# Two of 32 expert weight loads split into nine partition-strided DMAs

## The chip, the core and the metric

The kernel runs on one core of one Trainium2 chip. The metric is the device time of one execution in microseconds; a comparison takes medians of several runs. The core has a matrix engine (TensorE, PE in the profile), a vector engine (DVE), a scalar engine (ACT), GpSimd (POOL), a sync engine (SP) that here only issues loads, and 16 DMA engines that move data between HBM and the on-chip memory SBUF, which has 128 partitions.

## The reference, cut to what matters

One block of a transformer on 256 tokens of width 1024, all in float32: a mixer (two attentions, gates, an output projection, about the first fifth of the time) and then a mixture of 32 experts, of which each token takes 4. The kernel computes the experts one after the other, each on up to 64 gathered tokens, so it reads all weights of all experts once:

```python
def expert_block(args):
    xb, e = args
    hgu = xb @ w_gu[e] + b_gu[e]                     # w_gu[e]: 1024 x 2048 float32, 8 MB
    gate = jnp.minimum(hgu[:, :D_EXPERT], SWIGLU_LIMIT)
    up = jnp.clip(hgu[:, D_EXPERT:], -SWIGLU_LIMIT, SWIGLU_LIMIT)
    act = (up + 1.0) * gate * jax.nn.sigmoid(SWIGLU_ALPHA * gate)
    return act @ w_down[e] + b_down[e]               # w_down[e]: 1024 x 1024 float32, 4 MB
```

Here 1 MB is 2^20 bytes. 32 experts times 12 MB are 384 MB of the 436.72 MB (of 10^6 bytes) that the page counts, 402.7 of them in its unit.

## The kernel before

Program order is written out by hand for each engine. For expert `e` PE multiplies the gathered tokens with `w_gate_up` (line 1019, 64 matmuls), then with `w_down` (line 1033, 32 matmuls). Each of the two weights has two places in SBUF, one for even and one for odd experts: `gate_up_room`, and `even_down` / `odd_down`. A place is 128 partitions wide; for experts 6 to 27 partition `p` of a `w_down` place holds rows 8p to 8p+7 of the matrix, 32 KB that also lie in one piece in HBM (`dn_rows`).

SP issues all weight loads in one order: gate_up of expert e, then down of expert e, then e+1, and so on (`load_gate_up`, `load_down`). Before each it waits until PE has finished with expert e-2, which used the same place (`released`: semaphore `m_gu` for gate_up, `m_y` for down). Once a load has been issued it stands in the queue of the 16 DMA engines; SP goes on without waiting for its end.

A load says that it is done through a semaphore of its place (`full`), which rises by 16 per transfer. PE waits in `piece` until that semaphore has the sum of all transfers up to this expert; `full_count` computes the sum from `signals(e, i)`, the number of transfers for piece `i` of expert `e`. For `w_down` of experts 6 to 27 that number was 1 for the first half (`i == GU`) and 0 for the second, as one transfer brings both.

The middle of the program has a break before expert 16, where SP, DVE and ACT look at the largest token count of an expert, and where the biases of all experts are added. The last two experts' `w_down` come in halves and quarters, so that PE can begin before all has landed.

Of the kernel before, what the change touches and what calls it, by code (L numbers as in the profile page):

```python
# [25 lines left out]
P = 128  # L26
# [15 lines left out]
GU, DN = 4, 2  # L42
# [3 lines left out]
EIGHT = range(6, 28)  # L46
JOINED = tuple(e for e in range(6, 26) if e not in (15, 18))
BREAK = 16
OB = SEQ // SLOTS - 1
FF = 1024  # L50
EPS = 1e-6
# [86 lines left out]
def hybrid_block(nc, x, xt, w_in, gain_rows, head_rows, w_proj_a, w_proj_b, w_out,  # L138
                 w_router, w_gate_up, b_gate_up, w_down, b_down, consts, out):
    with ExitStack() as ctx:  # L140
# [208 lines left out]
        def whole_rows(e):  # L349

            return w_gate_up[0, e].rearrange("(p h) n -> p (h n)", h=KC)
# [12 lines left out]
        def dn_rows(e):  # L364

            return w_down[0, e].rearrange("(p h) n -> p (h n)", h=8)
# [9 lines left out]
        downs = [even_down[:, 0:8192], odd_down[:, 2048:10240]]  # L376

        def place(e, i):

            if i >= GU:  # L380
                return downs[e % 2][:, (i - GU) * 4096:(i - GU + 1) * 4096]
            return quads[e % 2 * 2 + i // 2][:, (i % 2) * 4096:(i % 2 + 1) * 4096]

        def full(e, i):
            return place_full[e % 2 * TURNS + i]

        def signals(e, i):

            if i < GU and e in JOINED:
                return 1 if i == 0 else 0  # L390
            if e in (WHOLE if i < GU else EIGHT):
                return 1 - i % 2
            return 2 if (e, i) in ((0, 5), (1, 4), (1, 5), (2, 0)) else 1

        def full_count(e, i):

            return 16 * sum(signals(n, i) for n in range(e % 2, e + 1, 2))

        def by_rows(e):

            return e != 0 and e != BREAK

# [24 lines left out]
        def _(sp):  # L427
# [33 lines left out]
            def load(e, i, done=None):  # L461
                sp.dma_start(place(e, i), source(e, i)).then_inc(done or full(e, i), 16)
# [28 lines left out]
            def released(e, i):  # L491

                if i < GU - 1:
                    sp.wait_ge(gu_used, (e - 2) * (GU - 1) + i + 1)
                elif i == GU - 1:
                    sp.wait_ge(m_gu, e - 1)
                elif i < TURNS - 1:
                    sp.wait_ge(dn_used, (e - 2) * (DN - 1) + i - GU + 1)
                else:
                    sp.wait_ge(m_y, e - 1)  # L500

            def load_gate_up(e):

                if e in JOINED:
                    released(e, GU - 1)
                    sp.dma_start(wholes[e % 2], whole_rows(e)).then_inc(full(e, 0), 16)
                    return
                for d in range(2):
                    if e in WHOLE:
                        released(e, 2 * d + 1)  # L510
                        load_quad(e, d)
                        continue
                    for i in (2 * d, 2 * d + 1):
                        if (e, i) == (2, 0):
                            sp.wait_ge(gu_first, 1)
                            load_half(e, i, 0)
                            released(e, i)
                            load_half(e, i, 1)
                        else:
                            released(e, i)  # L520
                            load(e, i)

            def load_down(e):

                if e in EIGHT:
                    released(e, TURNS - 1)
                    sp.dma_start(downs[e % 2], dn_rows(e)).then_inc(full(e, GU), 16)
                    return
                for i in range(GU, TURNS):
                    released(e, i)  # L530
                    load(e, i)
# [24 lines left out]

            for e in range(2, BREAK + 2):
                load_gate_up(e)
                load_down(e)
# [3 lines left out]
            with sp.If(most > SLOTS):  # L563
                for i in range(TURNS):
                    sp.wait_ge(full(BREAK, i), full_count(BREAK, i))
                with sp.Fori(0, NE) as e:
                    sp.wait_ge(o_pe, e * (6 * OB) + 1)
                    for i in range(GU):
                        sp.dma_start(place(BREAK, i), whole_rows(e)[:, i * 4096:(i + 1) * 4096]).then_inc(o_full, 16)
                    for s in range(DN):  # L570
                        sp.dma_start(place(BREAK, GU + s), dn_rows(e)[:, s * 4096:(s + 1) * 4096]).then_inc(o_full, 16)
                sp.wait_ge(o_pe, NE * 6 * OB + 1)
                for i in range(TURNS):
                    load(BREAK, i, o_full)

            for e in range(BREAK + 2, NE - 2):
                load_gate_up(e)
                load_down(e)
# [50 lines left out]
        def _(pe):  # L629
# [421 lines left out]
            def piece(e, i):  # L1051

                if signals(e, i):
                    pe.wait_ge(full(e, i), full_count(e, i))
                return place(e, i)
# [23 lines left out]
            def overflow():  # L1079

                with pe.Fori(0, NE) as e:
                    with pe.Fori(0, OB) as j:
                        n = e * OB + j
                        pe.wait_ge(o_dve, n * 5 + 1)
# [121 lines left out]
        def _(dve):  # L1206
# [425 lines left out]
            def overflow():  # L1632

                dve.wait_ge(m_gt, BREAK)
                with dve.Fori(0, NE) as e:
                    with dve.Fori(0, OB) as j:
                        n = e * OB + j
                        dve.wait_ge(o_pe, n * 6 + 1)
# [256 lines left out]
```

## Time and profile before

| | us |
|---|---|
| median of 3 runs (1127.17 to 1127.55) | 1127.24 |
| the profiled execution | 1131.17 |
| its span, first to last instruction | 1129.4 |
| PE busy | 1089.1 |
| DVE busy | 293.7 |
| ACT busy | 136.3 |

The profiled execution is 3.93 us longer than the median, and 1.8 us longer than its own span. The page cuts the span in 40 slices of 28.2 us; "DMA" is the mean busy share of the 16 DMA engines in tenths, "GB/s" what they moved, "PEclk" the granted TensorE clock. A PE that waits inside a stream of pipelined matmuls can still look busy, so a 9 in its line does not say that it sets the pace. "Landing" is the time from the issue of a transfer on SP to the last of its data.

### The profile page before, as it was taken

How to read it: one execution, taken by the hardware profiler on the slowest of the kernel's cores; microseconds unless marked ns; L12 is line 12 of the kernel's file. 1: busy time of each engine (PE TensorE's matmuls, PEld its weight loads, DVE VectorE, ACT ScalarE, POOL GpSimd, SP SyncE). 2: the span in 40 equal slices, each digit the busy share in tenths (PEclk: the TensorE clock that was granted, in tenths of full speed). 3: DMA queues.
4: the chain of work that ended last, by engine and by line, in shares of the span. 5: the costliest groups of instructions: out<-in, count | busy, mean ns of one | idle time of the engine just before them, and what ended most of it. 6: DMA issues, size and time to landing. Idle time of an engine off the chain costs nothing.

```text
span 1129.4 us, 11872 instructions
## 1 busy us (share of the span) xinstructions
PE 1089.1 (96%) x5275; PEld 481.4 (43%) x5275; DVE 293.7 (26%) x677; ACT 136.3 (12%) x232; POOL 8.3 (1%) x16
## 2 busy tenths in 40 slices
PE   9999999999999999999999968999999999999997
PEld 5678897533333333333333324333333333333332
DVE  2788742331111111121111110212111111111111
ACT  1425340110000000000000000100000000000001
POOL 0100000000000000000000000000000000000000
PEclk9999999999999999999999987999999999999999
DMA  8533488699999999999999999999999999999996
GB/s 313 231 150 138 161 319 357 263 400 402 430 428 438 439 430 425 435 435 428 435 430 424 436 420 426 430 429 436 427 433 430 433 432 430 431 424 428 427 424 261
DMA packets 21652, 436.72 MB, mean 387 GB/s; under 512 B 2496, under 2 KB 2880, under 8 KB 6272
## 3 DMA queue, kind: packets, MB, share of 16 engines
q1 hardware_dynamic: 21072, 435.27, 91.1%
q8 instruction: 43, 0.70, 0.3%
q10 hardware_dynamic: 528, 0.68, 0.2%
q14 instruction: 9, 0.07, 0.0%
HBM read 434.89 MB, written 1.05 MB: 386 GB/s over the span
## 4 chain that ended last, share of the span: by engine, by line
PE 79%; DMA 17%; DVE 3%; issue 1%; SPq 1%; ACT 0%; ACTq 0%; DVEq 0%
PE Pp L1019 33%; PE Bp L1033 14%; DMA gate_up_room<-in_w_gate_up 12%; PE Pp L701 4%; PE Ap L1047 4%; DMA odd_down<-in_w_down 3%; PE Bp L1005 3%; PE Pp L650 3%; PE Pp L666 2%; PE Pp L901 2%; PE Ap L912 2%; PE Bp L1026 1%; PE Pp L690 1%; DVE odd_down L1630 1%; DMA odd_down<-in_b_down 1%; PE Pp L961 1%
## 5 line engine op out<-in xcount | busy, mean ns | idle before, releaser
L1019 PE MATMUL Pp<-gate_up_room,OBT 128*64 128x512 f32 x2048 | 453.4, 601 | 13.8 <-DMA gate_up_room<-in_w_gate_up 13.8
L1019 PEld LDWEIGHTS Pp<-gate_up_room,OBT 128*64 128x64 f32 x2048 | 147.0, 139 | 303.7 <-issue 279.9
L1619 DVE TENSOR_SCALAR odd_down<-Pp 128x512 f32<-128x512 f32 x31 | 21.4, 692 | 618.2 <-PE Pp L1019 618.2
L1033 PE MATMUL Bp<-even_down,odd_down 128*64 128x512 f32 x512 | 113.7, 595 | 1.2
L1033 PE MATMUL Bp<-odd_down 128*64 128x512 f32 x480 | 106.3, 595 | 1.8 <-DVE odd_down L1630 0.6
L1820 ACT ACTIVATE odd_down<-odd_down 128x512 f32<-128x512 f32 x30 | 18.9, 630 | 476.0 <-DVE odd_down L1619 476.0
L1047 PE MATMUL Ap<-odd_down,cst 64*128 64x512 f32 x256 | 65.4, 630 | 5.2 <-DMA odd_down<-in_b_down 4.5
L1033 PEld LDWEIGHTS Bp<-even_down,odd_down 128*64 128x64 f32 x512 | 35.2, 137 | 69.1 <-issue 63.3
L1033 PEld LDWEIGHTS Bp<-odd_down 128*64 128x64 f32 x480 | 33.1, 137 | 65.3 <-issue 59.9
L1005 PE MATMUL Bp<-X,cst 128*64 128x512 f32 x240 | 56.6, 592 | 0.0
L701 PE MATMUL Pp<-odd_down,gate_up_room 128*128 128x128 f32 x448 | 53.2, 277 | 0.5 <-DVE odd_down L1370 0.5
L701 PEld LDWEIGHTS Pp<-odd_down,gate_up_room 128*128 128x128 f32 x448 | 51.1, 192 | 2.5 <-issue 1.3
L1832 ACT ACTIVATE odd_down<-Bp 128x512 f32<-128x512 f32 x30 | 17.9, 597 | 204.3 <-PE Bp L1033 204.3
L1047 PEld LDWEIGHTS Ap<-odd_down,cst 64*128 64x128 f32 x256 | 22.6, 190 | 46.2 <-issue 44.6
L650 PE MATMUL Pp<-gate_up_room,odd_down 128*128 128x512 f32 (+1 forms) x96 | 33.5, 507 | 0.0
L1630 DVE COPY odd_down<-Bp 128x512 f32<-128x512 f32 x31 | 21.4, 691 | 44.6 <-PE Bp L1026 44.6
L1005 PEld LDWEIGHTS Bp<-X,cst 128*64 128x64 f32 x240 | 17.1, 137 | 34.4 <-issue 34.4
L1026 PEld LDWEIGHTS Bp<-cst,odd_down 128*128 128x128 f32 x128 | 17.8, 208 | 26.3 <-DVE odd_down L1626 26.3
L666 PE MATMUL Pp<-odd_down,gate_up_room 128*128 128x256 f32 x128 | 28.2, 380 | 0.0
L912 PE MATMUL Ap<-gate_up_room,odd_down 128*128 128x512 f32 x64 | 28.1, 592 | 0.0
L1026 PE MATMUL Bp<-cst,odd_down 128*128 128x128 f32 x128 | 23.7, 307 | 3.2 <-DVE odd_down L1626 3.2
L666 PEld LDWEIGHTS Pp<-odd_down,gate_up_room 128*128 128x128 f32 x128 | 24.1, 190 | 3.5 <-issue 0.3
(227 smaller groups left out, 698.3 us busy)
## 6 DMA issues: line engine op xcount, KB each, us to landing
gate_up_room<-in_w_gate_up SPq DMA_DIRECT2D x14, 4096.0 KB, 23.6
gate_up_room<-in_w_gate_up SPq DMA_DIRECT2D x27, 2048.0 KB, 42.7
even_down<-in_w_down SPq DMA_DIRECT2D x11, 4096.0 KB, 36.0
odd_down<-in_w_down SPq DMA_DIRECT2D x11, 4096.0 KB, 39.6
gate_up_room<-in_w_in SPq DMA_DIRECT2D x8, 2048.0 KB, 7.4
even_down<-in_w_down SPq DMA_DIRECT2D x7, 2048.0 KB, 17.5
odd_down<-in_w_down SPq DMA_DIRECT2D x6, 2048.0 KB, 21.1
odd_down<-in_w_down SPq DMA_DIRECT2D x7, 1024.0 KB, 21.6
```

The lines of the kernel that those rows point to most:

```text
L650: last = mm(bank[:, 0:n], XT[:, k, b * P:(b + 1) * P], uview(u, n)[:, k, :], start=k == 0, stop=k == KC - 1)
L666: last = mm(bank[:, t * SEQ:(t + 1) * SEQ], uview(u)[:, k, c:c + P], XT[:, k, :], start=k == 0, stop=k == KC - 1)
L701: last = mm(Pp[:, t % 2, part * P:(part + 1) * P], w[:, k, f], x[:, k, :], start=start and k == 0, stop=stop and k == 3, skip_group_check= ...
L901: last = mm(Pp[:, c % 2, ab * SEQ:(ab + 1) * SEQ], urows(u)[:, j, c * P:(c + 1) * P], o[:, j, :], start=j == 0, stop=j == NP2 - 1)
L912: last = mm(Ap[:, 2 * b + hf, :], XT[:, c, b * P:(b + 1) * P], out_cols(hf)[:, c, :], start=c == 0, stop=c == KC - 1)
L1005: last = mm(out_bank[64 * r:64 * r + 64, :], OH[:, b, :], part, start=b == 0, stop=b == 1, skip_group_check=True)
L1019: last = mm((Gps, Ups)[q // 2][64 * (q % 2):64 * (q % 2) + 64, :], xT[:, k % 4, k // 4, :], quarter(e, w, q), start=False, stop=k == KC - ...
L1026: last = tr(bank[:, c * P:(c + 1) * P], act_fours[:, c, :], ident)
L1033: last = mm(bank[64 * hf:64 * hf + 64, :], turned[:, c, s, :], w[:, c * 1024 + hf * 512:][:, 0:512], start=s == 0 and c == 0, stop=s == DN ...
L1047: last = mm(Ap[:, 2 * b + hf, :], gates[h, b * P:(b + 1) * P], results[h, :], start=start, stop=stop, skip_group_check=True)
L1619: V.tensor_scalar(gm, Gps, LIMIT, None, ALU.min).then_inc(d_gm, 1)
L1630: V.tensor_copy(hTf, Yps).then_inc(d_ht, 1)
```

## The change

`w_down` of experts 12 and 22, both in `even_down`, no longer comes as one transfer of 128 rows (partitions) of 32 KB. It comes as nine: seven of 16 rows each, which take partitions r, r+8, r+16, ... for r from 0 to 6, and two of eight rows each, which take partitions 7, 23, 39, ... and 15, 31, 47, .... Together they write the same bytes to the same places. `signals` says 9 for these two, so PE waits for all nine. Everything else stands as it was; four lines go into `load_down`, and lines behind them move by 3 to 8.

```diff
--- before.py
+++ after.py
@@ -46,6 +46,7 @@
 EIGHT = range(6, 28)
 JOINED = tuple(e for e in range(6, 26) if e not in (15, 18))
 BREAK = 16
+UNEVEN = (12, 22)
 OB = SEQ // SLOTS - 1
 FF = 1024
 EPS = 1e-6
@@ -388,6 +389,8 @@
 
             if i < GU and e in JOINED:
                 return 1 if i == 0 else 0
+            if i == GU and e in UNEVEN:
+                return 9
             if e in (WHOLE if i < GU else EIGHT):
                 return 1 - i % 2
             return 2 if (e, i) in ((0, 5), (1, 4), (1, 5), (2, 0)) else 1
@@ -524,6 +527,11 @@
 
                 if e in EIGHT:
                     released(e, TURNS - 1)
+                    if e in UNEVEN:
+                        for first, step in [(r, 8) for r in range(7)] + [(7, 16), (15, 16)]:
+                            sp.dma_start(downs[e % 2][first:P:step, :], dn_rows(e)[first:P:step, :])\
+                                .then_inc(full(e, GU), 16)
+                        return
                     sp.dma_start(downs[e % 2], dn_rows(e)).then_inc(full(e, GU), 16)
                     return
                 for i in range(GU, TURNS):
```

On SP, around expert 12, the order before is this (`gate_up_room` and `even_down` / `odd_down` are the places, 128x8192 is partitions by float32 elements; the second row is `w_down` of expert 11, the third `w_gate_up` of expert 12):

```order
L506 DMA gate_up_room<-in_w_gate_up 128x16384
L527 DMA odd_down<-in_w_down 128x8192
L506 DMA gate_up_room<-in_w_gate_up 128x16384
L527 DMA even_down<-in_w_down 128x8192
L506 DMA gate_up_room<-in_w_gate_up 128x16384
L527 DMA odd_down<-in_w_down 128x8192
```

And this is the same place after the change:

```order
L509 DMA gate_up_room<-in_w_gate_up 128x16384
L535 DMA odd_down<-in_w_down 128x8192
L509 DMA gate_up_room<-in_w_gate_up 128x16384
L532 DMA even_down<-in_w_down 16x8192 x7
L532 DMA even_down<-in_w_down 8x8192 x2
L509 DMA gate_up_room<-in_w_gate_up 128x16384
L535 DMA odd_down<-in_w_down 128x8192
```

One transfer has become nine in the same place of the queue, between the gate_up loads of experts 12 and 13; at expert 22 it reads the same, between those of 22 and 23. No other engine's order moves.

## Rows read from the trace of the kernel before

**Rows 1.** The page, parts 1 to 3: engines, 40 slices of the span, DMA queues.

```profile
PE 1089.1 (96%) x5275; PEld 481.4 (43%) x5275; DVE 293.7 (26%) x677; ACT 136.3 (12%) x232; POOL 8.3 (1%) x16
PE   9999999999999999999999968999999999999997
DMA  8533488699999999999999999999999999999996
GB/s 313 231 150 138 161 319 357 263 400 402 430 428 438 439 430 425 435 435 428 435 430 424 436 420 426 430 429 436 427 433 430 433 432 430 431 424 428 427 424 261
q1 hardware_dynamic: 21072, 435.27, 91.1%
```

**Rows 2.** DMA view of 250 to 1113 us: busy tenths, packets, queues (packets, MB, share).

```profile
DMA  9999999999999999999999999999999999999999
DMA packets 13078, 370.21 MB, mean 429 GB/s; under 512 B 1467, under 2 KB 1467, under 8 KB 1625
q1 hardware_dynamic: 12945, 369.51, 99.9%
q8 instruction: 32, 0.52, 0.2%
```

**Rows 3.** Who waited for whom, PE, whole span: us in total, times, longest.

```profile
PE Pp L1019 <- DMA gate_up_room<-in_w_gate_up: 13.8, 8, 2.6
```

**Rows 4.** The chain that ended last, from 1060 us: start, length, what.

```profile
1074.31 38.72 DMA odd_down<-in_w_down
...
1113.17 1.94 PE Pp L1033 x8
1115.11 1.92 PE Ap L1047 x8
1117.03 5.33 PE Pp L1033 x24
...
1122.38 0.60 ACT odd_down L1869
...
1123.03 1.15 PE Ap L1047 x4
```

**Rows 5.** Timeline, last weight load of w_down: start, length, what, idle before it.

```profile
1121.11 0.33 PEld L1033 LDWEIGHTS Pp<-odd_down,OBT 128*64 128x64 f32 x4 [0.53 <-DMA odd_down<-in_w_down]
```

**Rows 6.** DMA view of 1096 to 1120 us, 40 slices of 0.6 us.

```profile
DMA  9999999999999999999999999999865554644321
```

**Rows 7.** Windows: start:end, length, engines' busy time, PEclk, DMA share, GB/s.

```profile
9.00:14.00 5.00, 5.00 (x12) 2.21 (x11) 1.54 (x4) 0.00 (x0) 0.00 (x0) 1.00 1.04 415
24.60:26.60 2.00, 2.00 (x13) 2.00 (x13) 0.00 (x0) 0.58 (x2) 0.00 (x0) 1.00 1.05 221
250.00:1113.00 863.00, 831.67 (x3922) 301.54 (x3916) 158.16 (x369) 67.46 (x123) 0.52 (x1) 0.98 1.00 429
1113.00:1121.00 8.00, 7.83 (x36) 2.61 (x36) 0.00 (x0) 0.16 (x1) 0.00 (x0) 1.00 0.42 170
```

**Rows 8.** Line 527, loads of a whole w_down, 4 MB each.

```profile
L527 SPq DMA_DIRECT2D even_down<-in_w_down x11: 327/327/328, 361.5 to 932.5; - x11
DMA to landing us min/median/max: 21.3/37.5/45.3
```

**Rows 9.** Line 467, halves of 1 MB, the last of them at the program's end.

```profile
L467 SPq DMA_DIRECT2D even_down<-in_w_down x6: 433/4236/4247, 157.8 to 1070.0; - x6
```

**Rows 10.** Line 484, loads of 256 KB to 32 partitions each.

```profile
L484 SPq DMA_DIRECT2D odd_down<-in_b_gate_up x3: 341/421/422, 22.2 to 23.1; - x3
DMA to landing us min/median/max: 3.4/4.3/5.1
```

**Rows 11.** Line 451, loads of 512 KB to 128 partitions: issue ns, first and last start.

```profile
L451 SPq DMA_DIRECT2D X<-in_x x2: 433/471/509, 4.5 to 5.0; - x2
DMA to landing us min/median/max: 8.7/9.1/9.5
```

## The prediction

> **What bounds the kernel now.** I read the page first: PE looks 96% busy and the granted clock is at nine tenths nearly everywhere, which would name PE. But the DMA line stands at 9 from the ninth slice to the last but one, and the loads move 425 to 439 GB/s in most of those slices [rows 1]. So I asked for the DMA view of 250 to 1113 us: all forty slices at 9, the load queue busy for 99.9% of sixteen engines' time, 429 GB/s [rows 2]. The queue never runs dry in 863 us. The waits say the same from PE's side in a softer way: PE is released by a gate_up load eight times [rows 3]. PE may catch up or fall back in between; the transfers stand in one line, and each microsecond that the line grows is a microsecond on its end.
>
> The end is where it counts. The chain of waits goes from PE's last expert over a transfer of 38.72 us (most of it standing in line) that lands at 1113, and then through the last `w_down` matmuls, results and output [rows 4]. In the timeline PE waits once more for weights just before 1121.11 [rows 5]: the last of the data lands at about 1121.1, and 8.3 us of work and output follow up to 1129.4. That tail stays.
>
> How the sixteen engines end is the second thing to see. In the view of 1096 to 1120 us the busy share is 9 up to 1113, falls to 5 within 1.5 us, stays at 4 to 6 until about 1118, then runs out [rows 6]. About half of the engines finish near 1114, the others 1118 to 1121. From 1113 to 1121 the mean share is 0.42 [rows 7], so the mean engine has 0.42 x 8 = 3.4 us left and ends at 1116.4. A perfect split would end the loads 4.7 us earlier; nothing that only moves bytes between engines can bring more. I read two eights: an early one whose last member is done at about 1115.6, and a late one done at 1121.1, a lead of 5.5 us (an estimate from the digits, good to 1 us).
>
> **The change, part by part.** First the issues. Two single issues of 0.33 us [rows 8] become eighteen, so SP is busy 8 x 0.33 = 2.6 us longer at each of the two places. A load lands a median of 37.5 us after its issue [rows 8] while 4 MB take 4.19/0.429 = 9.8 us, so about 28 us of other transfers stand ahead of it. Behind the nine on SP stands the gate_up load of the next expert; it is issued 2.6 us later and still joins a long line. Cost: zero. An issue can take 4.2 us when much is outstanding, as at the program's end [rows 9]. Eight such would be 34 us, but then because the line is full, and a full line is not a dry one. I leave zero; that bound enters only as a small part of the high side.
>
> Second, the bytes per engine. At 429 GB/s over sixteen engines one moves 26.8 GB/s, so a row of 32,768 bytes takes 1.22 us. Before, each engine has 8 rows: 9.8 us. After, the seven transfers of 16 rows give each engine 7 rows, and the other 16 rows come in two groups of 8, a row for each of eight engines. If both groups use the same eight engines, those have 9 rows and the others 7: +1.22 and -1.22 us per expert, +2.4 and -2.4 us for both experts. The Trainium skill, "DMA: Bandwidth & Descriptors", section "Why a DMA increments its semaphore by 16 and not by 1", says that a DMA from SP over 8 rows takes the eight lowest-numbered engines, so the same for all four groups; no row here names an engine, so whether those are the early eight I can only guess.
>
> Third, where the bytes go, the big term. All weight loads before write all 128 partitions at once. The trace has three that don't: the loads of `b_gate_up`, 256 KB to 32 partitions each [rows 10]. Issued from 22.2 to 23.1 us and landed 3.4 to 5.1 us later, the first is in at 25.6 and the third at 28.2: 1.3 us each. The two loads of 512 KB to 128 partitions [rows 11], issued at 4.5 and 5.0 us and landed 8.7 and 9.5 us later, come in at 13.2 and 14.5, also 1.3 us apart, with twice the bytes. The windows agree: 221 GB/s with all DMA engines busy (share 1.05) from 24.6 to 26.6 us, against 415 GB/s at share 1.04 from 9 to 14 us [rows 7]. Busy engines that move half as much are waiting for something on the side of the 32 partitions. A transfer to 16 partitions is not in the trace, strided or not. Bounds from the rows: full rate if what limits the 32 is that they are neighbours, and the stride of eight spreads the rows well; a quarter of the rate if it goes by the number of partitions (16 for 32 at half). I take half, the nearest row. A row then takes 2.44 us. An engine with 7 rows needs 17.1 instead of 9.8 us (+7.3), one with 9 rows 22.0 (+12.2); for both experts +14.7 and +24.4.
>
> The Trainium skill has a rule that speaks against this change: "SBUF — State Buffer", section "Door 1: The DMA port swizzle", lets bits 2 to 4 and 6 of the partition number choose one of 16 ports. By it a step of eight partitions reaches 8 of the 16 ports at a time (two engines on each), as 32 neighbouring partitions do, so half the rate; the 221 GB/s agree for the 32.
>
> The sum: the load line ends at the later of the late eight, 1121.1 + 14.7 = 1135.8, and the early eight, 1115.6 + 24.4 = 1140.0, if it is the early eight that get nine rows. That is 18.9 us later. Engines are not in step: where one is still in the transfer before or already in the next one, a pair does not collide, which takes off perhaps 1 us per expert; where the rows of the groups of eight meet the other engines' next rows, it adds about as much. I cancel these. The profiled execution goes from 1131.17 to 1150.1; from the median 1127.24 it is 1146.1 us.
>
> Nothing hides this. PE ahead of the loads does not help, since the line for loads is never empty; a PE that gets its weights later gives places free later, but by no more than the loads are late.
>
> **The rivals.**
>
> Split only, full rate. The strided rows collide nowhere and the early eight get the extra rows: late 1121.1 - 2.4 = 1118.7, early 1115.6 + 2.4 = 1118.0, so the loads end 2.4 us sooner and the time is 1124.8 us, faster. For it: the ends of the two eights fit almost too well (5.5 us of lead, 4.9 moved). Against it: a half rate at 221 GB/s [rows 7, 10]. It turns the sign where a strided row costs less than 1.14 times a row of before: there the 14 strided rows of the late eight cost 14 x 0.17 = 2.4 us more, which is what the two rows less give back. At full rate with the wrong eight it is 2.4 us slower, 1129.7; with the extra rows spread over all sixteen, 1127.2, a change that does not do what it says.
>
> Half rate, the late eight get nine rows. Then 1121.1 + 24.4 = 1145.5, 24.4 us later: 1151.6 us. For it: nothing tells which eight is which. Against: nothing either; I hold the early eight likelier only because the late ones must have other work (32 fetches of instructions stand in the queues [rows 2]), and small system work need not fall on the lowest numbers.
>
> Collisions in part. Engines out of step by several rows share ports only half of the time: a row at 1.5 times, 1.83 us. Seven rows 12.8 (+3.0), nine 16.5 (+6.7); for two experts +6.1 and 13.4 - 5.5 = +7.9: 1135.1 us. For it: at 1113 the engines are up to 7 us apart, some six rows. Against: the early and the late eight may each be close together, and only engines that share a port matter.
>
> Rate by number of partitions, a quarter. Nine rows at 4.88 us are 43.9, +34.1; twice, less the lead, +62.8: 1190 us. For it 32 partitions at half; against it, nothing but that the stride spreads over all the range. SP stuck in slow issues goes in here.
>
> **How the numbers follow.** Half rate, early eight: 0.56. Half rate, late eight: 0.12. In part: 0.12. A quarter or slow issues: 0.03. Full rate: 0.12 with the early eight, 0.03 with the late, 0.02 spread evenly. The likeliest is 1146.1, with its own range of 1141 to 1150. The range of 1131 to 1156 takes in the first three (0.80) with a margin of 3 to 4 us for the two unknown sizes. A measurement here tells a change from none at about 0.2%, 2.3 us. Faster: 0.12. Same: the even spread, and some of the two small cases that fall under 2.3 us: 0.05. Slower: 0.83.
>
> **What would show it.** In the DMA view of the stretch where expert 12's `w_down` is moved (547 to 562 us before; about 12 us longer after) and of expert 22's (840 to 856), DMA share near 1.00 with GB/s at 215 to 260 shows the collision; 429 kills it. The landing of an even `w_down` with 9 pieces would exceed its neighbours' by 7 to 12 us. At the end of the loads, the run-out of 8 us stays at about 7 (late eight 1133 to 1136, early eight 1138 to 1140) if I am right, with the eights in turned order; it shrinks to 3 us, ending near 1118.7, by the first rival, and grows to some 17 us if the late eight got nine rows. PE's own work per expert and SP's order stay as they are. The prediction is wrong if loads stay at 429 GB/s through both places, or if the delay at expert 12 is gone by expert 16, which would mean that the line ran dry somewhere before.

## The result

| | before | after |
|---|---|---|
| median of 6 runs, us | 1127.78 | 1164.24 (1159.23 to 1167.04) |
| profiled execution, us | 1131.17 | 1163.89 |
| its span, us | 1129.4 | 1161.8 |

The change makes the kernel slower by 36.5 us; the ratio is 1.0309, 95% interval 1.029 to 1.0329. The direction was forecast, but the forecast size was 18.9 us, about half of what came, and the range ended at 1156. So the mechanism has to be checked, and the terms of the sum with it. The ratios, here and below, leave out executions more than 1.5% above the fastest of the same kernel, while the medians take all.

The page of the changed kernel: PE, granted clock, busy share of the DMA engines, GB/s; each slice is 29.0 us.

```profile
PE   9999999999999999999869969999997799999997
PEclk9999999999999999999879988999999899999999
DMA  8534298699999999999999999999999999999995
GB/s 313 216 145 182 109 379 364 264 389 412 430 430 438 432 430 431 432 432 408 241 432 421 437 424 417 444 432 432 434 312 321 433 430 421 431 424 427 429 423 239
```

Against [rows 1] the DMA line is as full as it was. GB/s has one slice at 241 and two at 312 and 321 where it had 430 to 435: the loads of experts 12 and 22. The granted clock dips at both places (to 0.83 and 0.97 of full speed in the windows below, 1.00 before), where PE now waits; the time is set by the loads and not by PE, so this is not counted as a cost.

Windows of before around the two places (start:end, length, engines' busy time, clock, DMA share, GB/s), then the same windows after, with two inside the first place:

```profile
540.00:600.00 60.00, 55.62 (x269) 20.36 (x266) 11.28 (x26) 4.70 (x9) 0.00 (x0) 1.00 1.00 433
845.00:895.00 50.00, 49.83 (x242) 17.99 (x239) 9.00 (x20) 4.42 (x8) 0.00 (x0) 1.00 1.02 439
```

```profile
540.00:600.00 60.00, 43.68 (x190) 15.75 (x188) 8.16 (x21) 3.35 (x7) 0.00 (x0) 0.83 0.99 314
845.00:895.00 50.00, 43.87 (x204) 16.29 (x202) 10.25 (x24) 3.82 (x7) 0.00 (x0) 0.97 1.01 301
553.00:569.00 16.00, 14.72 (x58) 4.67 (x59) 0.00 (x0) 0.00 (x0) 0.00 (x0) 0.79 1.13 218
569.00:576.00 7.00, 6.89 (x36) 2.87 (x32) 3.45 (x7) 1.30 (x3) 0.00 (x0) 1.00 0.79 178
```

All engines busy and 218 GB/s while rows of the seven 16-row transfers are moved, half of the 429 of [rows 2, 7]; then 178 GB/s where the two groups of eight rows go, beside the first rows of the next load. (The share of such a short window swings about 1, here from 0.79 to 1.13, so its GB/s are rough too.) What a place loses can be read from the missing bytes: (433 - 314) x 60 / 429 = 16.6 us at expert 12, (439 - 301) x 50 / 429 = 16.1 us at expert 22. Their sum, 32.7 us, is the distance of the two profiled executions (1163.89 - 1131.17 = 32.7); that it is less than 36.5 us comes from the profiled execution of before, one of its longer ones. The tail behind the last load is as forecast, 8.3 us before and 1161.8 - 1153.3 = 8.5 us now (timeline of the changed kernel, PE's last wait for weights):

```profile
1153.31 0.14 PEld L1041 LDWEIGHTS Pp<-odd_down,OBT 128*64 128x64 f32 x2 [0.28 <-DMA odd_down<-in_w_down]
```

PE's waits in the changed kernel (total us, times, longest):

```profile
PE Pp L1027 <- DMA gate_up_room<-in_w_gate_up: 34.0, 8, 11.4
PE Bp L1041 <- DMA even_down<-in_w_down: 5.3, 2, 4.3
```

The waits for gate_up grow from 13.8 us [rows 3] to 34.0, with one of 11.4 us, and the `w_down` itself is waited for (5.3 us). SP's issues of the nine transfers:

```profile
L532 SPq DMA_DIRECT2D even_down<-in_w_down x18: 540/589/656, 519.6 to 840.2; - x18
```

They take 0.59 us each where a full load took 0.33 [rows 8], 10.6 us for eighteen. It is time that SP has: the loads stand in line for far longer than that.

The end of the loads, DMA busy share in 40 slices of 0.6 us from 1130 to 1154, the changed kernel first, then e1_even16 (below), which moves 8 rows on every engine:

```profile
DMA  9999999999999999999999888885322200111000
```

```profile
DMA  9999999999999997765555454300000000000699
```

Of before, the digits stood at 5 for a while, with half of the engines done [rows 6], and so they do in e1. In the changed kernel 8 falls to 2 within a few slices. The trace also has the time at which each of the 16 engines reported its part of the last load as landed. Before, eight did so from 1113.2 to 1115.7 us and eight from 1118.6 to 1121.1, as the prediction read it. In the changed kernel thirteen did by 1148.0 and the last three at 1150.1, 1152.6 and 1153.0; in e1 eight from 1139.2 to 1143.5 and eight from 1145.4 to 1147.0. So in the changed kernel the two eights are no longer apart. That fits nine rows going to the early eight, but the turned order that was forecast, with eight engines some 4 us behind the others, did not come.

The mean of the 16 last landings moves from 1116.9 to 1147.5 us, by 30.6, and the last one from 1121.1 to 1153.0, by 31.9.

### The profile page after: what moved, and what is told of

It reads as the page before. It is cut to its first block, busy times and chain, and to the rows that moved or that the text cites. A ratio compares the mean times of both kernels' runs of the same rounds, so it can differ in the third digit from the quotient of the medians.

```text
span 1161.8 us, 11888 instructions
## 1 busy us (share of the span) xinstructions
PE 1097.0 (94%) x5275; PEld 485.8 (42%) x5275; DVE 293.7 (25%) x677; ACT 136.3 (12%) x232; POOL 8.4 (1%) x16
## 4 chain that ended last, share of the span: by engine, by line
PE 76%; DMA 17%; DVE 3%; another core or an unknown queue 2%; SPq 2%; issue 1%; ACT 0%; ACTq 0%; DVEq 0%
PE Pp L1027 32%; PE Bp L1041 14%; DMA gate_up_room<-in_w_gate_up 8%; PE Pp L709 4%; DMA even_down<-in_w_down 4%; PE Ap L1055 4%; DMA odd_down<-in_w_down 4%; PE Bp L1013 3%; PE Pp L658 3%; PE Pp L674 2%; PE Pp L909 2%; PE Ap L920 2%; PE Pp L698 1%; PE Bp L1034 1%; DMA odd_down<-in_b_down 1%
## 5 line engine op out<-in xcount | busy, mean ns | idle before, releaser
L1027 PE MATMUL Pp<-gate_up_room,OBT 128*64 128x512 f32 x2048 | 459.2, 608 | 34.1 <-DMA gate_up_room<-in_w_gate_up 34.0
L1027 PEld LDWEIGHTS Pp<-gate_up_room,OBT 128*64 128x64 f32 x2048 | 149.4, 140 | 327.7 <-issue 284.5
L1828 ACT ACTIVATE odd_down<-odd_down 128x512 f32<-128x512 f32 x30 | 18.9, 630 | 502.9 <-DVE odd_down L1627 502.9
L1034 PEld LDWEIGHTS Bp<-cst,odd_down 128*128 128x128 f32 x128 | 17.8, 208 | 26.2 <-DVE odd_down L1634 26.2
L1034 PE MATMUL Bp<-cst,odd_down 128*128 128x128 f32 x128 | 23.7, 308 | 3.2 <-DVE odd_down L1634 3.2
```

The source lines that it names most:

```text
L1027: last = mm((Gps, Ups)[q // 2][64 * (q % 2):64 * (q % 2) + 64, :], xT[:, k % 4, k // 4, :], quarter(e, w, q), start=False, stop=k == KC - ...
L1034: last = tr(bank[:, c * P:(c + 1) * P], act_fours[:, c, :], ident)
```

## The experiments

Medians in us, ratio to the kernel before run beside it, 95% interval. Each edit is to the list of transfers in `load_down` (and the number in `signals`), for experts 12 and 22 unless said otherwise.

| run | w_down of 12 and 22 as | median | before | ratio |
|---|---|---|---|---|
| e1_even16 | 8 x 16 rows, stride 8 | 1157.42 | 1128.78 | 1.0269 [1.0232, 1.0306] |
| e2_columns | 9 x 128 rows, parts of the columns | 1129.9 | 1128.78 | 1.0014 [1.0003, 1.0025] |
| e3_near16 | 8 x 16 neighbours | 1170.32 | 1128.78 | 1.0394 [1.0353, 1.0435] |
| e4_helpers | 1 x 128 rows, 16 x 8 short rows | 1135.6 | 1128.78 | 1.0063 [1.0044, 1.0082] |
| e5_alternate | e1, order 0 4 1 5 2 6 3 7 | 1152.88 | 1127.3 | 1.021 [1.0184, 1.0236] |
| e6_near32 | 4 x 32 neighbours | 1157.93 | 1127.3 | 1.025 [1.0221, 1.0278] |
| e7_near32_crossed | e6, order 0 64 32 96 | 1160.25 | 1127.3 | 1.0261 [1.0222, 1.0301] |
| e8_only12 | the change at 12 alone | 1145.13 | 1127.3 | 1.0142 [1.0116, 1.0168] |
| e9_wide_narrow | 4 x 128 rows from 1 MB each | 1128.08 | 1129.02 | 0.9999 [0.9985, 1.0012] |
| e10_narrow_spread | 4 x 32 rows from all 4 MB | 1158.89 | 1129.02 | 1.0271 [1.0245, 1.0298] |
| e11_block12 | gate_up and down of 12, stride 8 | 1164.96 | 1129.02 | 1.0327 [1.03, 1.0355] |
| e12_stride2 | 2 x 64 rows, stride 2 | 1129.54 | 1129.02 | 1.0007 [0.9992, 1.0023] |
| e13_change_x6 | the change at six experts | 1256.62 | 1127.21 | 1.1037 [1.0946, 1.1128] |
| e14_even16_x6 | e1 at six experts | 1219.78 | 1127.21 | 1.0784 [1.075, 1.0818] |

### Is it the strided rows, and at what price? (e1, e2)

```diff
-for first, step in [(r, 8) for r in range(7)] + [(7, 16), (15, 16)]:
+for first, last, step in [(r, P, 8) for r in range(8)]:                                  # e1, signals 8
+for a, b in [(896 * i, 896 * i + 896) for i in range(8)] + [(7168, 8192)]:  # columns    # e2, signals 9
```

> The two 8-row transfers become an eighth transfer of 16 rows (partitions 7, 15, ...), so every DMA engine again moves 8 rows; still strided by eight. Theory A (strided rows share ports two by two, and the groups of eight rows did extra harm on top, by meeting other engines' loads): a row costs 2.44 us, 8 x 1.22 = 9.8 us more per expert, 19.5 for both: about 1147 to 1149. Theory B (what costs is the number of small transfers, about 36/18 = 2 us each): 16 transfers instead of 18, about 1160. Theory C (a strided row simply costs three times a row, 2 x 2 x 9.8 = 39 us): 1164 or more, no better than the change.

> The same w_down loads in nine transfers as well, but each over all 128 partitions and a ninth of the columns. Theory A: all ports in use all the time, nothing to pay, 1127.8 within 1.5 us. Theory B (number of transfers): about 1164.

e2: nine transfers as such cost 1.1 to 1.6 us together. Theory B falls. e1 costs 28.6 us (30.3 by the ratio), between A's 20 and C's 39: with even bytes on the engines the loss is already more than the whole forecast. Its windows:

```profile
540.00:600.00 60.00, 43.99 (x195) 15.21 (x195) 7.58 (x20) 3.19 (x6) 0.00 (x0) 0.86 1.00 340
845.00:895.00 50.00, 42.69 (x198) 15.17 (x194) 10.25 (x24) 4.42 (x8) 0.00 (x0) 0.96 1.00 303
```

Missing bytes: 13.0 and 15.9 us, where eight rows at twice the price make 9.8. So there are 3 to 6 us at each place that the price of the strided rows does not hold.

Where they go can be read from the durations of single packets in the trace, where each packet of a load is one row moved by one engine. Before the change, a row of 32 KB takes 1.22 us and a 64 KB row of a `w_gate_up` load 2.42 us. In e1 a strided row takes 2.2 to 2.7 us for the most part, and rows of the full `w_gate_up` loads beside them get slower too, up to 5.9 us; in the changed kernel they reach 4.9 us just ahead of the strided rows and 7.1 us just behind. The time above that of before, summed over the packets and divided by 16 engines, at expert 12 and at expert 22 (windows 530 to 605 and 820 to 900 us):

| us per engine, at 12 / at 22 | 32 KB rows, the strided ones among them | 64 KB rows of the loads beside |
|---|---|---|
| changed kernel | 11.0 / 10.5 | 4.3 / 4.9 |
| e1_even16 | 9.8 / 10.1 | 2.7 / 4.4 |
| e12_stride2 (below) | 0.0 / 0.0 | 0.0 / 0.0 |

For the changed kernel the four numbers sum to 30.7 us, the 30.6 us by which the mean landing moved. So a strided row costs about twice a row of before, and the rest is paid by full loads next to it.

### Which side of the transfer? (e9, e10)

```diff
+for r in range(4):   # e9: all partitions, a quarter of the columns, from 1 MB of HBM
+    piece = w_down[0, e, 256 * r:256 * r + 256, :].rearrange("(p h) n -> p (h n)", h=2)
+    sp.dma_start(downs[e % 2][:, 2048 * r:2048 * r + 2048], piece).then_inc(full(e, GU), 16)
+for r in range(4):   # e10: 32 partitions, rows of HBM from everywhere
+    sp.dma_start(downs[e % 2][32 * r:32 * r + 32, :], dn_rows(e)[r:P:4, :]).then_inc(full(e, GU), 16)
```

> Separates the two sides of a transfer. w_down of experts 12 and 22 comes as four transfers, each writing all 128 partitions (a quarter of the columns, 8 KB a row) from one piece of 1 MB in HBM, the same span of HBM that a transfer of e6_near32 reads; the rows of the matrix come in another order, so these two experts' results are not the reference's. If the loss is made at the on-chip memory's side: none here, 1127 to 1130. If reading from a narrow span of HBM makes it: as e6, 1158.

> The other half: four transfers of 32 neighbouring partitions as in e6_near32, but each reads every fourth row of HBM, over the whole 4 MB; again with another order of rows for the two experts. On-chip side: as e6, 1158 within 4 us. HBM side: 1127 to 1135.

Both bring the rows of the two matrices in another order, so their results are not those of the reference; the bytes and the work are the same. e9's windows, then e10's:

```profile
540.00:600.00 60.00, 55.48 (x257) 19.58 (x258) 11.11 (x29) 4.80 (x9) 0.00 (x0) 0.97 1.01 431
845.00:895.00 50.00, 49.55 (x238) 17.75 (x236) 10.25 (x24) 4.42 (x8) 0.00 (x0) 1.00 1.02 440
```

```profile
540.00:600.00 60.00, 42.15 (x178) 13.86 (x176) 5.12 (x12) 2.80 (x5) 0.00 (x0) 0.83 1.01 330
845.00:895.00 50.00, 42.56 (x194) 15.42 (x190) 10.24 (x24) 4.41 (x8) 0.00 (x0) 0.93 1.00 294
```

431 and 440 against 330 and 294 GB/s. Reading from 1 MB or from all 4 MB of HBM made no difference in this pair; which partitions are written at a time did.

### Which partitions? (e3, e5, e6, e7, e12)

```diff
+for first, last, step in [(16 * r, 16 * r + 16, 1) for r in range(8)]:             # e3
+for first, last, step in [(r, P, 8) for r in (0, 4, 1, 5, 2, 6, 3, 7)]:            # e5
+for first, last, step in [(32 * r, 32 * r + 32, 1) for r in range(4)]:             # e6
+for first, last, step in [(r, r + 32, 1) for r in (0, 64, 32, 96)]:                # e7
+for first, last, step in [(r, P, 2) for r in range(2)]:                            # e12
```

> Eight transfers of 16 neighbouring partitions instead of strided ones. Theory A, with the port map of the Trainium skill's page SBUF - State Buffer (4 ports for 16 neighbours), says a quarter of the rate, 4.88 us per row, +29.3 us per expert, about 1186. If any 16 partitions are as good as any other 16, it equals e1_even16, whatever that is (about 1147).

> The same eight transfers of 16 strided rows as e1_even16 (1157.4 us, +28.6), issued in the order r = 0, 4, 1, 5, 2, 6, 3, 7 instead of 0 to 7. Theory A (which ports of the memory a transfer reaches decides; by the port map of the Trainium skill's page SBUF - State Buffer r = 0 to 3 reach one set of eight ports and r = 4 to 7 the other): in e1 the sixteen engines stay on the same eight ports for four rows each, so being out of step does not help; here an engine that is a row behind its partner uses the other set, so a good part of the collisions go away: +10 to +20 us, 1139 to 1149. Rival (the cost belongs to small, strided transfers as such, to the strided reads of HBM, or to any 16 partitions): the order makes no difference, 1157 within 3 us.

> Four transfers of 32 neighbouring partitions, in the order 0, 32, 64, 96; HBM is read in one piece each. Theory A: the first two reach one set of eight ports, the last two the other, as in e1_even16: +24 to +29 us, 1152 to 1158. Rival (strided access or the number of transfers costs): nothing is strided and there are 8 transfers instead of 16, so at most half of e1's loss, 1143 or less.

> As e6_near32 with the order 0, 64, 32, 96. Theory A: engines that are out of step by two rows or more now use different sets of ports; less than e6, by 5 to 12 us. Rival: equal to e6.

> Two transfers of 64 rows, every second partition. Together their 64 partitions reach all sixteen ports of the map in the Trainium skill's page on SBUF. If the engines take the rows in blocks of four neighbours of the list, engines share ports at each moment as in e1 and it costs the same, 1150 to 1158; if a transfer that reaches all ports is free, 1127 to 1131.

e6 met theory A: 32 neighbours cost what 16 rows strided by eight cost (1.025 and 1.0269), with half the transfers and nothing strided. e3 is dearer than both, so not any 16 partitions are alike, but it did not reach a quarter of the rate: 41.5 us instead of 58. e5 seems to have gained something (23.7 to 25.6 us lost instead of 28.6, though the intervals of the two ratios just touch), less than half of what I had expected; e7 gained nothing, and there theory A was wrong about the effect of order. A reason that fits e5 and e7 is that engines a few us apart (4.8 us from first to last at expert 12 before) do not slip past each other where a turn on one set of ports takes 4.9 us (two rows at 2.44), but partly do where it takes one row. It was not tested by itself.

e12 was a surprise. Its windows:

```profile
540.00:600.00 60.00, 54.94 (x256) 19.27 (x254) 10.54 (x27) 4.41 (x8) 0.00 (x0) 0.97 1.00 431
845.00:895.00 50.00, 49.83 (x242) 18.00 (x240) 9.09 (x20) 4.41 (x8) 0.00 (x0) 1.00 1.01 434
```

431 and 434 GB/s: two transfers of 64 rows, every second partition, are free. So a transfer need not be 128 partitions wide. That it is the spread over the partitions and not the number 64 that makes it free is not shown by this run alone, since 64 neighbours were not tried; that the number does not decide by itself is shown by e1 and e3, both of 16. By the page "SBUF — State Buffer", section "Door 1: The DMA port swizzle" (the Trainium skill), a step of two reaches all sixteen ports, a step of eight only eight at a time, 32 neighbours eight, 16 neighbours four. The order of the measured losses (0, 28.6, 30.6, 41.5 us) agrees. No run here shows which engine wrote which partition.

### Is anything given back later? (e8)

```diff
-UNEVEN = (12, 22)
+UNEVEN = (12,)
```

> The change at expert 12 alone. If the loss is made at each place and nothing gives it back later, half of 36.5 us: 1144 to 1148. If the line of loads ran dry in the break before expert 16, or PE's faster stretch behind it, took it up, less: 1128 to 1140.

17.8 us (16.0 by the ratio), half of the change's loss. Windows at expert 12, at 22, and between:

```profile
540.00:600.00 60.00, 37.97 (x166) 13.28 (x164) 5.12 (x12) 2.81 (x5) 0.00 (x0) 0.83 1.00 314
845.00:895.00 50.00, 47.74 (x222) 16.84 (x220) 10.24 (x24) 4.42 (x8) 0.00 (x0) 0.97 1.00 432
600.00:840.00 240.00, 226.05 (x1056) 85.00 (x1052) 41.76 (x99) 17.46 (x32) 0.53 (x1) 0.96 1.00 430
```

The loss stands at expert 12 only; behind it the line moves at 430 GB/s, through the break before expert 16 too. The line did not run dry there, so nothing was regained.

### What the price of the rows leaves out (e11)

```diff
+UNEVEN = (12,)
+for r in range(8):   # gate_up of expert 12 too, just ahead of its w_down
+    sp.dma_start(wholes[e % 2][r:P:8, :], whole_rows(e)[r:P:8, :]).then_inc(full(e, 0), 16)
```

Its `w_down` goes in the same eight transfers as in e1, and `signals` says 8 for each of the two loads.

> Expert 12 alone, but both of its loads, gate_up (8 MB) and w_down (4 MB), one behind the other, each in eight transfers of 16 rows strided by eight. If the loss is twice the price of a row inside, plus a part that is paid once where strided and full loads meet (about 3 to 5 us per block): 12 MB x 2.44 us = +29.3, and +4, 1159 to 1163. If a strided byte simply costs what e1_even16 showed per load, 14.3 us for 4 MB: +43, 1170.

35.9 us for one block of 12 MB. The window 500 to 620 of this kernel:

```profile
500.00:620.00 120.00, 79.30 (x356) 27.57 (x354) 15.37 (x36) 6.62 (x12) 0.00 (x0) 0.82 1.00 304
```

Before, the same window had 431 GB/s, so (431 - 304) x 120 / 429 = 35.5 us, again the measured loss. With e1, 14.3 us for a block of 4 MB, two equations: 8x + m = 14.3 and 24x + m = 35.9 give x = 1.35 us more per row and m = 3.5 us per block. With x held at 1.22, the price of a doubled row, m is 4.5 from e1 and 6.6 from e11. Either way the loss is a bit more than double rows plus a part of 3.5 to 6.6 us that is paid once per block. The two runs fix that part only roughly, since e1's interval is 26 to 35 us for its two places. That it does not grow with the bytes of the block follows with e14 (below): there a place costs 14.1 to 15.4 us by the interval, three times that is 42 to 46, and e11's interval is 34 to 40. Its main share is what the table of packet times under e1 shows for the full loads on both sides of the block, 2.7 and 4.4 us there. Full rows are slow where some engines still have, or again have, a full load while others are in the strided one.

### The groups of eight (e13, e14, e4)

```diff
-UNEVEN = (12, 22)
+UNEVEN = (8, 10, 12, 14, 20, 22)          # e13 with the nine transfers, e14 with e1's eight
```

> The change at six experts (8, 10, 12, 14, 20, 22) instead of two. If each place costs what it does at two (36.5/2 = 18.2 us), +109 us, about 1237. Of that, if it is the imbalance of bytes that counts, the eight engines with nine rows fall behind the others by 2.4 us a place, so the loads end with a long run-out, up to 9 us between the last engine and the mean; if the groups of eight collide with everybody's loads, the run-out stays near 8 us in all and every engine is late.

> The eight transfers of 16 strided rows of e1_even16 at the same six experts, 8 rows for every engine. If each place costs what it does at two (28.6/2 = 14.3 us), +86 us, about 1214. The distance to e13_change_x6 is six times what the two groups of eight rows cost beyond an eighth transfer of 16: 23 us if the 3.9 us per place of the separate comparisons are right; 10 us or less if the difference between them was mostly noise and the run-out's.

By the ratios e13 loses 116.9 us, 19.5 a place, and e14 88.4 us, 14.7 a place, both close to the cost at two places (18.2 and 14.3). e13's ratio rests on only two executions, 1236.73 and 1253.38 us; its other two took 1259.86 and 1276.3. The intervals are apart, so it is likely that the two groups of eight cost more than an eighth transfer of 16 rows. How much more is open: 28.5 us or 4.8 a place by these ratios, but at two places 3.9 by the medians and 1.9 in the mean of the engines, where the missing bytes of the change exceed e1's by (16.6 + 16.1) - (13.0 + 15.9) = 3.8 us.

Whether the cause is imbalance or collisions is not shown. In both profiled executions one engine lands its last data far behind all others, by 19 us in e13 and by 18 us in e14, where the bytes are even. The lag is made at the places: the `w_gate_up` loads of the next expert behind 10, 12 and 14 land 11, 18 and 35 us apart from the first to the last engine in e13, and 7, 14 and 22 in e14. By the loads of expert 19 the distance is down to 8 us in both, and in one slice shortly before the DMA engines are less than 80% busy in both; probably the others waited there for the late one. So with six places the line is not full throughout, and part of what these two runs lose is this one engine's. What singles it out no run shows.

```diff
+sp.dma_start(downs[e % 2][:, 0:7168], dn_rows(e)[:, 0:7168]).then_inc(full(e, GU), 16)      # e4, signals 17
+for a in (0, 64, 32, 96):
+    for r in range(4):   # eight rows, every fourth partition, the last 1024 columns
+        part = slice(a + r, a + 32, 4)
+        sp.dma_start(downs[e % 2][part, 7168:8192], dn_rows(e)[part, 7168:8192]).then_inc(full(e, GU), 16)
```

> The bytes per engine are as uneven as in the change (9 and 7 rows' worth), but nearly free of shared ports: 7168 of 8192 columns go in one 128-partition transfer, the last 1024 columns in sixteen transfers of eight rows, every fourth partition, 4 KB a row. If engines are the limit, the end moves by -2.4 us when the lowest eight are the early ones (1125.4) and by +2.4 when they are the late ones (1130.2). If ports are the limit, nothing can be gained, since each port takes its 8 rows whichever engine writes them, and the helpers' rows hold up the helped: 1128 to 1133.

6.8 us slower, more than either theory gave. Moving the same bytes between engines this way gains nothing. The loss of 7 us was not foreseen, but the packets show where it is: the 64 KB rows of the loads beside take up to 4.2 us instead of 2.42, the 28 KB rows of the wide transfer up to 2.1 us where most take 1.07, and the 4 KB rows 0.22 to 0.25 us, where an eighth of a 32 KB row's time is 0.15. Together that is about 3 us per engine at each place. No version beat the kernel before, and none of the runs points to one.

## Why the prediction was wrong

What bounds: right. The line of loads is never empty, it sets the end, and what it loses is not given back (e8).

The issues: right that they cost nothing here, though one takes 0.59 us and not 0.33. In e2 one issue even held SP for 18.6 us, in a kernel that loses 1.1 to 1.6 us in all.

The price of a row: right in the main. Twice, taken from the nearest row of the trace, the `b_gate_up` loads at 221 GB/s [rows 7, 10]; 218 GB/s were measured inside the place, and e9 and e10 put the cause on the partitions written. The first rival, a pure shift of bytes at full rate, falls with e1.

The step that failed is in the sum: "which takes off perhaps 1 us per expert; where the rows of the groups of eight meet the other engines' next rows, it adds about as much. I cancel these." Being out of step takes nothing off. It makes the full `w_gate_up` loads on both sides of the strided rows slow, a row of theirs up to 7.1 us instead of 2.42, and that costs 4.3 and 4.9 us per engine at the two places, 9.2 us for which the sum has zero. That strided and full rows then share a port is the likeliest reason; no run shows which port a row used. The 32 KB rows themselves cost 21.5 us per engine for both places, where the forecast has (14.7 + 24.4) / 2 = 19.5 in the mean: short by 2.0. These two make up the miss in the mean engine, 30.6 us measured against 19.5.

The lead of the early eight, -5.5 us in the sum, was real (the landings above show it). It bought less than forecast: the eights closed up, but the last engine ends 5.5 us behind the mean, where it was 4.2 before and would have been 3.6 by the forecast. Together 9.2 + 2.0 + 1.9 = 13.1 us, against the 13.0 us by which the last landing's 31.9 us exceed the forecast 18.9. How much of this is owed to the groups of eight is known only in part: at each place the change costs the mean engine 1.9 us more than e1 does.

The range could have been told wider from the rows: bounds of a half and a full rate were taken for the strided rows, but none for the loads beside them.

## What to carry to other kernels

When 16 DMA engines are the limit, ask of each transfer which partitions it writes at one time. All 128, or every second of them, run at full rate; 32 neighbours, or 16 at a stride of eight, run at half, 16 neighbours lower still, and the transfers before and behind pay too, some 3 to 7 us per block here. Splitting along the columns is nearly free (0.14% for 18 transfers). Uneven ends of the engines (8 us here from the first to the last) look like a gain to be had by moving rows; here both ways that were tried (the change and e4) cost more.

## What was not expected of the hardware

Two transfers of 64 rows at every second partition cost nothing (1.0007 [0.9992, 1.0023]). Sixteen neighbours at a time cost 41.5 us and not the 58 of a quarter of the rate. Windows of e3_near16, the first inside its place:

```profile
553.00:565.00 12.00, 11.80 (x44) 3.72 (x46) 0.00 (x0) 0.00 (x0) 0.00 (x0) 0.80 0.99 171
540.00:600.00 60.00, 38.15 (x166) 13.36 (x164) 5.12 (x12) 2.81 (x5) 0.00 (x0) 0.83 1.00 294
```

171 GB/s is 0.40 of 429, where four engines on each port in use would make 0.25.

How long an issue keeps SP goes by the shape and not only by the number of rows: 0.33 us for 128 rows, 0.42 for 16 or 32 neighbours (e3, e6), 0.43 for 128 rows of a part of the columns (e2, e9), and 0.57 to 0.62 (medians) wherever partitions are skipped, with 64 rows (e12) as with 16 (e1) or eight (e4).

Loads to few partitions slow full loads that are beside them in the line, a 64 KB row from 2.42 to as much as 7.1 us.
